# State-space setups moved within the first FFN of a hybrid decoder trunk, B and C loaded earlier, one scan split

## The chip, the cores and the metric

The kernel runs on one core of one Trainium2 chip. The metric is the device time of one execution in microseconds (us). A core has five engines that run side by side, each through its own list of instructions: TensorE (PE, matmuls; PEld is its weight load), VectorE (DVE), ScalarE (ACT), GpSimd (POOL) and SyncE (SP), which here only issues transfers. They wait for each other through semaphores, which are counters: an instruction adds to one when it is done, and another engine waits for a value.

## The reference

A trunk of two layers over 1024 tokens of width 1024, batch 1, float32. Cut to what matters:

```python
x = x + even_mixer(rms_norm(x, ...))                  # RWKV-7 and RG-LRU
x = x + conv_ffn(rms_norm(x, f_norm_g[0]), ...)       # "the first FFN"
x = x + odd_mixer(rms_norm(x, ...))                   # S5, below
x = x + conv_ffn(rms_norm(x, f_norm_g[1]), ...)
return rms_norm(x, final_norm_g)

def conv_ffn(xn, w_up, conv_w, conv_b, w_down):       # 1024 -> 2 x 2816 -> 1024
    h = causal_dwconv(xn @ w_up, conv_w, conv_b)
    gate, val = jnp.split(h, 2, axis=-1)
    return (silu(gate) * val) @ w_down

def odd_mixer(xn, w_in, A_re, A_im, log_dt, B_re, B_im, C_re, C_im, D, w_glu):
    u = xn @ w_in                                     # 64 groups of 16 channels
    a = exp((A_re + i A_im) * dt)                     # 64 complex states per group
    b_bar = (a - 1) / (A_re + i A_im) * (B_re + i B_im)
    s[t] = a * s[t - 1] + b_bar u[t]                  # over 1024 tokens
    y = gelu(Re((C_re + i C_im) s) + D * u)
    val, gate = jnp.split(y @ w_glu, 2, axis=-1)
    return val * sigmoid(gate)
```

## The kernel before, in words

Every matmul in float32 is done in three: weights and activations are each split in a high part (a ScalarE cast) and a low part (the rest, by GpSimd for weights, by VectorE for activations), and high x high, high x low and low x high are added in PSUM.

**The first FFN, up phase.** 22 pairs (i = 0 to 21), each a tile of 128 gate and 128 value columns. A pair is made by a seven-product scheme (`ORDER`, `part_pe`): 84 matmuls of 128x512. Pairs use two sets of PSUM banks in turn. The raw weights come by SP (`load_raw`, L2084), GpSimd makes sums of blocks, ScalarE the high parts (`w_hi_act`, L2107), GpSimd the low parts (`w_lo_pool`, L2111). VectorE adds the pieces and scales them (`evac_dve`, L2633), does the convolution (`conv_dve`, L2610) and the product of gate and value (`h_dve`, L2617). The finished hidden tile is stored in HBM (`hidden_sp`). Behind its own work of pair i, VectorE calls `beside_pair_dve`. Each engine works through its list in order: ScalarE's casts of the next weights stand behind its work on the evacuated banks (`begin_act`, L2375).

**The first FFN, down phase.** Hidden tiles come back from HBM (`fetch_sp`) in four groups of 7, 5, 5 and 5. In each group there are eight units (c = 0 to 7), one for each 128 output columns; a unit of group 0 is 7 x 3 x 2 = 42 matmuls of 128x512 into one of two accumulators in turn (L2257). Units 0 and 1 take their weights in two chunks (`load_chunk`, L2289), the others by `load_down` (L181), with casts (L2402, L191) and low parts (L2337, L198), all a unit ahead. After unit c VectorE adds the accumulator to the residual (L2689), splits one hidden tile for the next group (L2391), and calls `beside_dve(g, c)`.

**The state-space tables** are built beside this FFN by the class `Tables`. VectorE's steps are small, mostly on 128x32, and linked: most wait for the one before. `angles_dve(0)` copies D and an identity (20 copies, counted in `s5_clear`); `setup_dve` 0 and 1 make powers of a, 2 the factor of B, 3 `b_bar` (needs B), 4 the starts of the turning tables, 5 and 6 double those tables (`fine`, `coarse`), 7 clears two buffers and `powers_dve(0)` begins the filters. C comes by SP (`load_c_sp`), is transposed by TensorE after units 3 and 5 of group 0 (`turn_c_pe`, L2805) and copied by VectorE (`keep_c`). In groups 1 and 2 each unit carries one of 16 halves of the filters: GpSimd multiplies (`half_products_pool`, L3043, into t_mg) and sums (`half_sums_pool`, L3053, into t_gx), VectorE makes t_hx (L3099, L3109), TensorE transposes and multiplies (`half_pe`, L3121 to L3135), ScalarE keeps the result, and it goes to HBM.

**The S5 layer.** For each of eight tiles i TensorE does state matmuls (`states_pe`, L3522), filter matmuls (`filters_pe`) and output matmuls (`output_pe`, L3545), between units of the input projection. Ahead of `states_pe(i)` stand three waits: `unit_free`, `in_read` (the transfer g_in of tile i has landed, L3410) and `s5_dve` at 15 * (i - 1) + 5. VectorE's scan of a tile is 15 counted instructions: one copy, four products, an addition, a subtraction, two scans (L3751), four products, two sums. After scan 5 it also makes the low parts of four tiles of y (`g_part`, L3367).

The order of all this is written out by hand. SP's list around the change is in `load_sp`, GpSimd's in `lo_pool`.

Of the kernel before, what the change touches and what calls it, by code (L numbers as in the profile page):

```python
# [61 lines left out]
def trunk(nc, io, out):  # L62
# [1840 lines left out]
    NP = FT  # L1903
# [15 lines left out]
    class Ffn:  # L1919
# [381 lines left out]
        def load_sp(self, sp):  # L2301
            for i in range(1, NP):
                for n in ("11", "22", "12", "21"):
                    self.load_raw(sp, i, n)
                if i > 1:
                    self.hidden_sp(sp, i - 2)
            self.load_chunk(sp, 0, 0)
            for m in range(self.groups[0][1]):
                self.fetch_sp(sp, m)
            self.hidden_sp(sp, NP - 2)  # L2310
            self.load_chunk(sp, 0, 1)
            for g in range(len(self.groups)):
                fetched = list(self.next_tiles(g))
                if g:
                    self.load_chunk(sp, g, 0)
                    self.load_chunk(sp, g, 1)
                    for m in fetched[:3]:
                        self.fetch_sp(sp, m)
                    fetched = fetched[3:]
                for c in range(2, DT):  # L2320
                    self.load_down(sp, g, c)
                    if (g, c) == (0, 2):
                        self.hidden_sp(sp, NP - 1)
                        if self.tables:
                            self.tables.load_first_sp(sp, self.q_used0 + SEVEN * NP)
                    for m in fetched[:2]:
                        self.fetch_sp(sp, m)
                    fetched = fetched[2:]
                    if (g, c) == (0, 5) and self.tables:
                        self.tables.load_second_sp(sp)  # L2330
# [439 lines left out]
    class Tables:  # L2770
# [47 lines left out]
        def beside_pair_dve(self, dve, i):  # L2818
            if i == 2:
                self.angles_dve(dve, 0)  # L2820
            elif i in (4, 6):
                self.angles_dve(dve, i // 2 + 1)
            elif i in (8, 9, 10):
                self.setup_dve(dve, i - 8)
            elif i == 11:
                self.setup_dve(dve, 4)

# [4 lines left out]
        def beside_first_pool(self, pool, g, c):  # L2832
            if self.half_of(g, c) is not None:
                self.half_products_pool(pool, self.half_of(g, c))

        def beside_pool(self, pool, g, c, lo_done):
            if self.half_of(g, c) is not None:
                self.half_sums_pool(pool, self.half_of(g, c), lo_done)
            elif g > self.HALF_GROUPS[-1] and c in (2, 3):
                self.turns_pool(pool, 0, c - 2)  # L2840
# [21 lines left out]
        def beside_dve(self, dve, g, c):  # L2862
            if g == 0 and c == 1:
                self.setup_dve(dve, 5)
            elif g == 0 and c == 2:
                self.setup_dve(dve, 6)
            elif g == 0 and c == 3:
                self.setup_dve(dve, 3)
            elif g == 0 and c in (4, 6):
                self.keep_c(dve, c // 2 - 2)  # L2870
            elif g == 0 and c == 5:
                nc.vector.memset(t_gx[:, :, :, :, :], 0.0).then_inc(s5_clear, 1)
            elif g == 0 and c == 7:
                self.setup_dve(dve, 7)
# [85 lines left out]
        def double_turns(self, table, n, size):  # L2960
# [9 lines left out]
            self.square_turn()  # L2970

        def setup_dve(self, dve, c):
            run = self.link.run
# [34 lines left out]
            elif c == 4:  # L3008
# [5 lines left out]
                for _ in range(3):  # L3014
                    self.square_turn()
            elif c == 5:
                for table in (fine, coarse):
                    run(nc.vector.memset(table[:, 0, :, 0:1], 1.0))
                    run(nc.vector.memset(table[:, 1, :, 0:1], 0.0))
                for n in (1, 2, 4, 8):  # L3020
                    self.double_turns(fine, n, 16)
            elif c == 6:
                for n in (1, 2, 4):
                    self.double_turns(coarse, n, 8)
            else:
# [6 lines left out]
        def half_products_pool(self, pool, n):  # L3032
# [7 lines left out]
            if n == 0:  # L3040
                pool.wait_ge(s5_clear, 23)
            for k, (b, a) in enumerate(((0, 0), (1, 1), (1, 0), (0, 1))):
# [156 lines left out]
    with ExitStack() as sc:  # L3199
# [182 lines left out]
        with nc.Block() as block:  # L3382
# [315 lines left out]
            def _(dve):  # L3698
# [28 lines left out]

                def scan_dve(i):
                    done = 15 * i

                    def up(ins):
                        ins.then_inc(s5_dve, 1)

                    c_i, s_i = (rot[i % 2][:, :, k, :] for k in range(2))
# [10 lines left out]
                    dve.wait_ge(s5_dve, done + 4)  # L3745
                    up(nc.vector.tensor_tensor(x, x, xt, ALU.add))
                    dve.wait_ge(s5_dve, done + 5)
                    up(nc.vector.tensor_tensor(y, y, yt, ALU.subtract))
# [23 lines left out]
                for i in range(DT):  # L3772
                    scan_dve(i)
                    if i + 2 < DT:
                        scale_u(i + 2)
                    if i == DT - 3:
                        for k in range(4):
                            g_part(nc.vector, k, y_lo_dve)
# [47 lines left out]
```

## Time and profile before

| | us |
|---|---|
| median of 3 runs | 2570.85 (2568.71 to 2570.9) |
| profiled execution | 2569.76 |
| its span in the trace | 2566.3 |
| TensorE busy in it | 2461.1 (96%) |
| VectorE, ScalarE, GpSimd busy | 1463.5, 1108.4, 1307.2 |

The span is from the first to the last instruction in the trace. Times in rows are microseconds from its start. The up phase of the first FFN lies before 1204, group 0 of its down phase from there to 1289, groups 1 to 3 up to 1514, and the S5 scan ends near 1700.

### The profile page before, as it was taken

To read this page: it belongs to the slowest core of one execution; us is meant where nothing else is said; L and a number is where in the kernel's file an instruction comes from. 1 tells how busy PE (TensorE), PEld (TensorE's weight loads), DVE (VectorE), ACT (ScalarE), POOL (GpSimd) and SP (SyncE) were. 2 spreads that over 40 slices of the span, in tenths; PEclk is the share of its full clock that TensorE was granted. 3 is DMA by queue.
4 is the path that set the end of the run, shared out by engine and by line. 5 is a ranking of instruction groups with operands and counts; after the bars stand their busy time and mean duration, and the time that the engine had idled before them with its cause. 6 is when DMAs were issued, how large, how long until landed. Compare 5 with 4: busy or idle time off the path is not lost. (4 is left out here: it accounts for less than half of the span.)

```text
span 2566.3 us, 33658 instructions
## 1 busy us (share of the span) xinstructions
PE 2461.1 (96%) x12861; PEld 2049.7 (80%) x12861; DVE 1463.5 (57%) x1902; ACT 1108.4 (43%) x1782; POOL 1307.2 (51%) x1072
## 2 busy tenths in 40 slices
PE   8999899999999998999999999989999999999997
PEld 6788788888777786888778878978878888888886
DVE  6441578877556667566566546654375565562223
ACT  5442344544444543455144444433265454452222
POOL 5323445454246775875268644412367777762221
PEclk9999999999999999999999999999999999999998
DMA  3112000000111222223445424531212222243312
GB/s 107 46 39 60 21 1 2 1 1 1 42 58 58 91 74 66 83 85 126 116 167 201 139 90 144 174 106 54 61 49 88 78 82 90 75 140 107 111 50 86
DMA packets 249504, 203.46 MB, mean 79 GB/s; under 512 B 25061, under 2 KB 228359, under 8 KB 247303
## 3 DMA queue, kind: packets, MB, share of 16 engines
q1 hardware_dynamic: 235143, 179.63, 22.4%
q10 hardware_dynamic: 14208, 21.76, 2.4%
q8 instruction: 99, 1.62, 0.3%
q14 instruction: 54, 0.44, 0.1%
HBM read 148.92 MB, written 48.23 MB: 77 GB/s over the span
## 5 line engine op out<-in xcount | busy, mean ns | idle before, releaser
L198 POOL TENSOR_TENSOR dense_lo<-dense_raw,dense_hi 128x512 fp32r<-128x512 f32 (+2 forms) x142 | 175.4, 1236 | 465.9 <-ACT dense_hi L191 465.6
L191 ACT CAST dense_hi<-dense_raw 128x512 fp32r<-128x512 f32 (+2 forms) x142 | 79.3, 565 | 393.1 <-PE acc_o L1716 144.2
L2111 POOL TENSOR_TENSOR dense_lo<-w_raw_l,dense_hi 128x512 fp32r<-128x512 f32 x88 | 118.2, 1343 | 63.9 <-ACT dense_hi L2107 63.7
L2111 POOL TENSOR_TENSOR dense_lo<-w_sums_l,dense_hi 128x512 fp32r<-128x512 f32 x66 | 103.1, 1563 | 72.9 <-ACT dense_hi L2107 72.9
L2111 POOL TENSOR_TENSOR w_l<-w_raw_l,w_l 128x512 fp32r<-128x512 f32 x88 | 114.9, 1305 | 46.7 <-ACT w_l L2107 46.7
L198 POOL TENSOR_TENSOR w_lo_e<-w_raw_e,w_hi_e 128x512 fp32r<-128x512 f32 x42 | 56.4, 1345 | 158.1 <-ACT w_hi_e L191 158.1
L404 PE MATMUL main_ps<-rounded 128*128 128x256 f32 x896 | 128.1, 294 | 8.9 <-DVE rounded L299 8.9
L404 PEld LDWEIGHTS main_ps<-rounded 128*128 128x128 f32 x896 | 113.6, 190 | 27.3 <-DVE rounded L299 23.3
L2111 POOL TENSOR_TENSOR w_l<-w_sums_l,w_l 128x512 fp32r<-128x512 f32 x66 | 104.0, 1575 | 45.1 <-ACT w_l L2107 45.1
L2257 PE MATMUL bank_b<-h_hi_l,dense_hi 128*128 128x512 f32 x352 | 109.9, 394 | 6.2 <-POOL dense_lo L198 5.8
L2173 PE MATMUL acc_o<-x_early_l,dense_hi 128*128 128x512 f32 x352 | 108.7, 390 | 3.4 <-POOL dense_lo L2111 3.4
L2173 PE MATMUL bank_a<-x_early_l,w_l 128*128 128x512 f32 x396 | 104.5, 400 | 7.4 <-POOL w_l L2111 7.4
L2257 PE MATMUL bank_b<-h_lo_l,dense_hi 128*128 128x512 f32 x352 | 109.3, 392 | 0.0
L2257 PE MATMUL bank_b<-h_hi_l,dense_lo 128*128 128x512 f32 x352 | 108.8, 391 | 0.0
L2173 PE MATMUL acc_o<-x_late_l,dense_hi 128*128 128x512 f32 x352 | 108.3, 389 | 0.0
L2633 DVE TENSOR_TENSOR bank_b<-bank_b,p_kept_later_l 128x512 f32<-128x512 f32 x44 | 28.5, 695 | 139.8 <-ACT p_kept_later_l L2367 139.8
L2257 PE MATMUL bank_a<-h_hi_l,dense_hi 128*128 128x512 f32 x336 | 105.2, 394 | 2.0 <-DVE h_lo_l L2391 1.3
L2689 DVE TENSOR_TENSOR x_res<-x_res,bank_a 128x1024 f32<-128x1024 f32 x28 | 34.2, 1220 | 126.8 <-PE bank_a L2257 126.8
L2173 PE MATMUL bank_a<-x_late_l,w_l 128*128 128x512 f32 x396 | 104.0, 399 | 1.2 <-DVE x_late_l L2071 1.2
L2257 PE MATMUL bank_a<-h_lo_l,dense_hi 128*128 128x512 f32 x336 | 103.7, 390 | 0.0
L2257 PE MATMUL bank_a<-h_hi_l,dense_lo 128*128 128x512 f32 x336 | 103.5, 389 | 0.0
L2173 PE MATMUL acc_o<-x_early_l,w_l 128*128 128x512 f32 x396 | 100.9, 390 | 2.0 <-ACT p_kept_l L2367 1.9
(545 smaller groups left out, 7035.4 us busy)
## 6 DMA issues: line engine op xcount, KB each, us to landing
w_raw_l<-in_f_w_up SPq DMA_DIRECT2D x176, 256.0 KB, 3.0
hidden<-val SPq DMA_DIRECT2D x44, 512.0 KB, 2.6
h_f_l<-hidden SPq DMA_DIRECT2D x44, 512.0 KB, 4.7
w_raw_e<-in_e_w_in SPq DMA_DIRECT2D x42, 256.0 KB, 2.9
dense_raw<-in_f_w_down SPq DMA_DIRECT2D x40, 256.0 KB, 2.9
dense_raw<-in_f_w_down SPq DMA_DIRECT2D x48, 192.0 KB, 2.6
s_states<-t_hx ACTq DMA_DIRECT2D x16, 512.0 KB, 2.9
s_inputs<-t_in ACTq DMA_DIRECT2D x16, 512.0 KB, 3.0
```

The lines of the kernel that those rows point to most:

```text
L191: nc.scalar.copy(self.hi[:, par, 0:n, :], self.raw[:, par, 0:n, :]).then_inc(w_hi_done, 1)
L198: pool.tensor_tensor(self.lo[:, par, 0:n, :], self.raw[:, par, 0:n, :], self.hi[:, par, 0:n, :].bitcast(F32), op=ALU.subtract).then_inc(w_ ...
L404: return nc.tensor.matmul(bank[:, at:at + 2 * CH], lhs, rhs, skip_group_check=True, **flags)
L2111: pool.tensor_tensor(self.ring_lo[n % 4], self.source(ORDER[n % SEVEN]), self.ring_hi[n % 4].bitcast(F32), op=ALU.subtract).then_inc(q_lo, 1)
L2173: last = nc.tensor.matmul(bank, w[n % 4][:, j, :], x(j, BLOCK[k]), start=begins and j == 0 and w is self.ring_hi and x == self.x_hi, stop= ...
L2257: last = nc.tensor.matmul(self.down_acc[s][:, h * HALF:(h + 1) * HALF], place[w][:, t, :], x[here][:, h * HALF:(h + 1) * HALF], start=begi ...
L2633: nc.vector.tensor_tensor(here, here, kept, ALU.mult if kept.shape[-1] == SEQ else ALU.add).then_inc(q_evac, 1)
L2689: nc.vector.tensor_tensor(here, here, self.down_acc[c % 2][:, :], ALU.add).then_inc(unit_free, 1)
```

## The change

- SP: C (real part) and B are loaded right after unit 1's second weight chunk of group 0, and no longer after the last hidden store.
- VectorE: `angles_dve(0)` leaves pair 2, and setups 0, 1, 2 and 4 leave pairs 8, 9, 10 and 11. In group 0, unit 1 now carries setups 0 and 1, unit 2 setups 2 and 3, unit 3 the angle copies, the clearing of t_gx and setup 4, units 4 to 6 the former setups 5 and 6 in pieces beside the copies of C; unit 7 is as before.
- GpSimd: the products of the first half come after the low parts of unit 7 in group 0, and wait for 21 counts of `s5_clear` in place of 23.
- S5 scan: the scan of each tile is two functions, called one after the other; for tile 6 the low parts 2 and 3 of y come between them, and only 0 and 1 ahead.

```diff
@@ load_sp
             self.load_chunk(sp, 0, 1)
+            if self.tables:
+                self.tables.load_first_sp(sp, self.q_used0 + SEVEN * NP)
...
                     if (g, c) == (0, 2):
                         self.hidden_sp(sp, NP - 1)
-                        if self.tables:
-                            self.tables.load_first_sp(sp, self.q_used0 + SEVEN * NP)
@@ beside_pair_dve
-            if i == 2:
-                self.angles_dve(dve, 0)
-            elif i in (4, 6):
+            if i in (4, 6):
                 self.angles_dve(dve, i // 2 + 1)
-            elif i in (8, 9, 10):
-                self.setup_dve(dve, i - 8)
-            elif i == 11:
-                self.setup_dve(dve, 4)
@@ beside_first_pool, beside_pool
-            if self.half_of(g, c) is not None:
+            if self.half_of(g, c):
                 self.half_products_pool(pool, self.half_of(g, c))
...
+            elif (g, c) == (self.HALF_GROUPS[0] - 1, DT - 1):
+                self.half_products_pool(pool, 0)
@@ beside_dve
+            if g:
+                return
+            if c in (1, 2):
+                self.setup_dve(dve, 2 * c - 2)
+                self.setup_dve(dve, 2 * c - 1)
+            elif c == 3:
+                self.angles_dve(dve, 0)
                 nc.vector.memset(t_gx[:, :, :, :, :], 0.0).then_inc(s5_clear, 1)
+                self.setup_dve(dve, 4)
+            elif c == 4:
+                self.keep_c(dve, 0)
+                self.first_turns_dve()
+                for n in (1, 2, 4):
+                    self.double_turns(fine, n, 16)
+            elif c == 5:
+                self.double_turns(fine, 8, 16)
+                for n in (1, 2):
+                    self.double_turns(coarse, n, 8)
+            elif c == 6:
+                self.keep_c(dve, 1)
+                self.double_turns(coarse, 4, 8)
+            elif c == 7:
                 self.setup_dve(dve, 7)
                 self.powers_dve(dve, 0)
@@ half_products_pool
-                pool.wait_ge(s5_clear, 23)
+                pool.wait_ge(s5_clear, 21)
@@ vector list of the S5 layer
-                    scan_dve(i)
+                    scan_first_dve(i)    # copy, four products, addition
+                    if i == DT - 2:
+                        for k in range(2, 4):
+                            g_part(nc.vector, k, y_lo_dve)
+                    scan_rest_dve(i)
                     if i + 2 < DT:
                         scale_u(i + 2)
                     if i == DT - 3:
-                        for k in range(4):
+                        for k in range(2):
                             g_part(nc.vector, k, y_lo_dve)
```

`first_turns_dve` holds the four memsets that began setup 5.

## Rows read from the trace of the kernel before

**Rows 1.** The page's first part: busy time, share, instructions.
```profile
span 2566.3 us, 33658 instructions
PE 2461.1 (96%) x12861; PEld 2049.7 (80%) x12861; DVE 1463.5 (57%) x1902; ACT 1108.4 (43%) x1782; POOL 1307.2 (51%) x1072
```

**Rows 2.** Stretches of the up phase: length; busy PE, PEld, DVE, ACT, POOL; clock; DMA.
```profile
814.22:855.15 40.93, 38.66 (x170) 31.38 (x168) 27.91 (x42) 20.80 (x31) 28.01 (x23) 1.00 0.23 72
920.78:960.85 40.07, 38.67 (x170) 31.38 (x168) 26.97 (x42) 18.71 (x30) 28.30 (x23) 1.00 0.25 79
960.85:1008.49 47.64, 41.78 (x170) 33.35 (x168) 35.21 (x67) 18.52 (x29) 28.75 (x23) 0.93 0.21 67
1008.49:1051.55 43.06, 39.98 (x170) 32.59 (x168) 29.80 (x42) 19.14 (x29) 31.08 (x25) 0.96 0.23 74
1051.55:1089.63 38.08, 38.08 (x170) 31.54 (x168) 22.24 (x23) 19.11 (x28) 29.81 (x23) 1.00 0.27 84
```

**Rows 3.** Timeline behind setup 1: start, length, instruction, [idle before it and its releaser].
```profile
962.70 4.10 DVE L2895 TENSOR_TENSOR small<-power 128x32 f32<-128x32 f32 x4
...
972.59 1.20 ACT L2375 ACTIVATE gate<-acc_o,prm 128x1024 f32<-128x1024 f32 x1 [8.56 <-DVE acc_o L2633]
...
976.19 2.93 PE L2173 MATMUL bank_a<-x_early_l,w_l 128*128 128x512 f32 x6 [4.30 <-POOL w_l L2111]
```

**Rows 4.** Timelines of SP, ScalarE and TensorE in group 0.
```profile
1200.47 1.39 SPq L2289 DMA_DIRECT2D dense_raw<-in_f_w_down  x2
1212.06 4.97 SPq L181 DMA_DIRECT2D dense_raw<-in_f_w_down  x2
...
1219.30 1.51 SPq L2782 DMA_DIRECT2D c_raw<-in_o_C_re  x2
...
1224.29 3.08 SPq L2790 DMA_DIRECT2D b_raw<-in_o_B_im  x2
...
1230.61 0.98 SPq L181 DMA_DIRECT2D dense_raw<-in_f_w_down  x2
...
1219.55 0.62 ACT L191 CAST dense_hi<-dense_raw 128x512 fp32r<-128x512 f32 x1 [2.10 <-PE bank_a L2257]
...
1235.63 1.16 ACT L191 CAST dense_hi<-dense_raw 128x512 fp32r<-128x512 f32 x2 [11.49 <-DMA dense_raw<-in_f_w_down]
...
1237.73 0.78 PE L2257 MATMUL bank_b<-h_hi_l,dense_hi 128*128 128x512 f32 x2 [4.68 <-POOL dense_lo L198]
```

**Rows 5.** Timelines of GpSimd, VectorE and TensorE after group 0 ends at 1289.06.
```profile
1292.94 3.33 POOL L3043 TENSOR_TENSOR t_mg<-b_bar,power 128x256 f32<-128x256 f32 x4 [2.23 <-DVE t_fir L3029]
...
1295.82 3.49 DVE L3109 TENSOR_TENSOR t_hx<-t_mh 64x288 f32<-64x288 f32 x4
...
1299.95 1.97 PE L3121 MATMUL acc_o<-ident,t_gx 128*128 128x128 f32 x8 [2.77 <-POOL t_gx L3053]
```

**Rows 6.** Scan of tile 6: timelines; last, transfers from 1668 (count, KB, us to landing).
```profile
1670.82 0.58 SPq L3410 DMA_DIRECT2D g_in<-s_inputs  x1
...
1674.08 1.27 DVE L3744 TENSOR_TENSOR r_tmp<-bank_a,rot 128x512 f32<-128x512 f32 x2
...
1678.84 5.29 PE L3522 MATMUL bank_a<-u_now,g_in 128*128 128x128 f32 x32 [3.23 <-DVE f_hat L3751]
...
g_in<-s_inputs SPq DMA_DIRECT2D x1, 1024.0 KB, 7.9
```

**Rows 7.** Stretches behind two of the stalls, columns as in the second group.
```profile
1299.70:1303.10 3.40, 3.15 (x15) 3.16 (x16) 1.61 (x4) 1.33 (x4) 2.20 (x4) 0.51 0.48 158
1678.60:1681.90 3.30, 3.06 (x14) 3.09 (x15) 3.23 (x6) 0.00 (x0) 0.00 (x0) 0.50 0.41 101
```

**Rows 8.** Stretches of group 0 between residual additions of units 1, 3 and 7.
```profile
1223.57:1249.23 25.66, 20.98 (x87) 16.86 (x86) 18.02 (x77) 3.22 (x6) 4.54 (x4) 0.93 0.68 169
1249.23:1289.06 39.83, 39.83 (x185) 33.16 (x183) 16.98 (x20) 8.22 (x12) 8.98 (x8) 1.00 0.21 56
```

**Rows 9.** Sum over five stretches: angle copies and setups 0, 1, 2, 4.
```profile
sum 32.42, PE 32.42 PEld 26.88 DVE 30.17 ACT 6.64 POOL 17.70; mean PE 6.48 PEld 5.38 DVE 6.03 ACT 1.33 POOL 3.54
```

More of the change, by code:

```diff
@@ L2862, in beside_dve @@
         def beside_dve(self, dve, g, c):
[L2863 to L2871, printed above, removed]
-                nc.vector.memset(t_gx[:, :, :, :, :], 0.0).then_inc(s5_clear, 1)
-            elif g == 0 and c == 7:
+            if g:
[5 more added lines that the diff above has]
+                self.angles_dve(dve, 0)
+                nc.vector.memset(t_gx[:, :, :, :, :], 0.0).then_inc(s5_clear, 1)
+                self.setup_dve(dve, 4)
[12 more added lines that the diff above has]
+            elif c == 7:
                 self.setup_dve(dve, 7)
@@ L2970, in double_turns, with first_turns_dve @@
             self.square_turn()
+        def first_turns_dve(self):
+            for table in (fine, coarse):
+                self.link.run(nc.vector.memset(table[:, 0, :, 0:1], 1.0))
+                self.link.run(nc.vector.memset(table[:, 1, :, 0:1], 0.0))
         def setup_dve(self, dve, c):
@@ L3015, in setup_dve @@
                     self.square_turn()
[L3016 to L3024, printed above, removed]
             else:
@@ L3726, in scale_u, with scan_up, scan_first_dve @@
                     nc.vector.tensor_tensor(acc, acc, spread[:, :], ALU.mult).then_inc(u_scaled, 1)
[L3728 to L3732, printed above, removed]
+                def scan_up(ins):
+                    ins.then_inc(s5_dve, 1)
+                def scan_first_dve(i):
+                    done, up = 15 * i, scan_up
                     c_i, s_i = (rot[i % 2][:, :, k, :] for k in range(2))
@@ L3746, in scan_dve, with scan_rest_dve @@
                     up(nc.vector.tensor_tensor(x, x, xt, ALU.add))
+                def scan_rest_dve(i):
+                    done, up = 15 * i, scan_up
+                    c_i, s_i = (rot[i % 2][:, :, k, :] for k in range(2))
+                    x, y = f_hat[:, 0, :, :], f_hat[:, 1, :, :]
+                    xt, yt = r_tmp[:, 0, :, :], r_tmp[:, 1, :, :]
                     dve.wait_ge(s5_dve, done + 5)
```

## The prediction

> **What bounds the kernel now.** The page's first part comes first: TensorE is busy for 2461.1 of 2566.3 us [rows 1]. No other engine can be the bound as a whole, so the only time to win is the 105 us in which TensorE stands still, plus whatever its clock loses after standing. The next view is therefore TensorE's timeline with the idle time ahead of each row, and the stretches cut so that each holds equal work. The reader is to see four places.
>
> (a) Up phase. Two pairs of tiles are 168 matmuls and take 38.08 us where nothing disturbs them (170 records: the cuts take in both ends). Four other stretches with the same 170 records take 40.93, 40.07, 47.64 and 43.06 us [rows 2]. They are the pairs beside which VectorE runs the angle copies (pair 2), setup 0 (pair 8), setups 1 and 2 (pairs 9, 10) and setup 4 (pair 11). The timeline shows how: four products of setup 1 take 4.10 us, the evacuation behind them ends late, ScalarE sits 8.56 us before it may start the gate tile, its next weight cast is queued behind that, GpSimd waits for the cast, and TensorE stands 4.30 us [rows 3].
>
> (b) First down group, fourth unit. TensorE stands 4.68 us for a low part, ScalarE's cast before it 11.49 us for weights from HBM, and SP had issued these only at 1230.61, because C and B (from 1219.30) and two fetches were ahead of them [rows 4].
>
> (c) Edge of groups 0 and 1. TensorE stands 2.77 us for t_gx, whose products GpSimd began only at 1292.94, after VectorE's two memsets [rows 5].
>
> (d) Scan. TensorE stands 3.23 us before the state matmuls of tile 7 [rows 6]. The view names VectorE's scan. I read this one differently, below.
>
> Each long stall is followed by a stretch at a granted clock of 0.5, the lower of the two levels (1.2 GHz); after (c) and (d) it lasts 3.4 us [rows 7]. Such a stretch costs half its length if TensorE is busy in it.
>
> **The change, part by part.**
>
> *Setups out of the up phase.* Angle copies and setups 0, 1, 2, 4 leave pairs 2 and 8 to 11. What they cost is read from whole stretches, so that stall and low clock are both in it: 40.93 - 38.08 = 2.85; 40.07 - 38.08 = 1.99; 47.64 - 38.08 = 9.56; 43.06 - 38.08 = 4.98 [rows 2]. Sum 19.38 us, all on the path, as TensorE is followed at once by the next pair. The angle steps beside pairs 4 and 6 stay, so nothing is counted for them. I take 19.4; the bounds are 17 (a rest of short waits stays) and 19.4.
>
> *B and C ahead of the third unit's weights.* Six loads move on SP from behind the last hidden store to ahead of the weights of unit 2. Their condition (all up-phase low parts made) is met by then. In the trace the queue issues nothing there: the second weight chunk is out by 1201.9, and unit 2's first load comes at 1212.06, when GpSimd has freed its buffer [rows 4]. The six took from 1219.30 to 1227.4, 8.1 us, so they fit the 10.2 us gap. Behind them come unit 2's weights, the last hidden store and fetches of tiles 7 and 8, some 8 us earlier than now, and unit 3's weights, then released by GpSimd's low part of unit 2. So the DMA wait goes. Price of the stall with its slow clock: from the residual addition of unit 1 to that of unit 3 are 25.66 us [rows 8]. Two units of 42 matmuls at 38.08/168 = 0.2267 us are 19.04. Gain 6.6 us. What could be late instead are unit 2's weights, now behind the small packets. Unit 3's, behind the same packets and two fetches, were cast 5.0 us after their issue; at that rate unit 2's are there at 1217.1, for a cast at 1219.55 [rows 4]. Bounds of this part: 4 and 6.6.
>
> *VectorE in group 0.* This is the place where the moved work is paid. The five steps took 32.42 us in the up phase, with GpSimd busy for 17.70 us of that in 17 instructions [rows 9]. There a VectorE instruction on two operands in SBUF ends only when GpSimd's ends (four products of 32 columns in 4.10 us [rows 3]); one short instruction of 0.19 us still slips through per GpSimd instruction. Without GpSimd they are 32.42 - 17.70 + 17 x 0.19 = 17.9 us. What VectorE does now between the two ends of group 0 is 18.02 + 16.98 = 35.0 us [rows 8]. With the moved work 52.9, and some 1.5 for short gaps between linked steps: 54.4. After the gain above, the group is 65.5 - 6.6 = 58.9 us long. Spare: 4.5 us, against GpSimd's part there. GpSimd is busy 8.98 of 39.83 us there, in eight instructions of 1.1 us [rows 8]: two low parts for each unit, one in its middle, one under the residual addition, which reads PSUM and isn't held up. Six of the first kind lengthen VectorE's work by 6 x 1.1 = 6.6 at most. So VectorE ends group 0 between 4.5 early and 2 late (at the up phase's rate: 32.42 + 35.0 + 1.5 - 58.9 = 10.0 late). TensorE feels a late residual addition only a unit later, as two accumulators alternate, and the second set of C transposes, which waits for VectorE's copies of the first, comes after unit 5, when by the same durations the copies are some 3 us old. I take no stall inside the group.
>
> The Trainium skill, "SBUF — State Buffer", section "SBUF: two separate sides", says that VectorE and GpSimd share a port pair as an exclusive lock, and that the loser is blocked for the other's whole instruction. The rows on VectorE's products agree. By that rule alone the six instructions cost 6.6 us and VectorE would be 2 us late, which the next step absorbs in part.
>
> *First half of the filters.* Its products go into GpSimd's gap after the low part of unit 7 and wait for 21 counts, not for the two memsets. They took 3.33 us beside VectorE [rows 5], and GpSimd has such gaps, as just counted. Only the sums are left at the edge; they end some 5 us after it, while TensorE comes 8.1 us after it (1297.18 = 1299.95 - 2.77). Late next is VectorE's t_hx, needed 1.1 us (eight transposes) after TensorE comes, that is 9.2 after the edge. It ended 10.25 after it (1299.31), and GpSimd's products and sums ran beside it; with the 3.33 us of products gone it gains half to all of them, so it ends 6.9 to 8.6 after the edge, plus any lateness. Gain 2.77 + 3.4/2 = 4.4 [rows 5, 7], less 0.6 for lateness. Taken 3.8, bounds 0 and 4.4.
>
> *Scan of tile 6 in two parts.* The state matmuls of tile 7 wait for s5_dve at 95, which is the copy and four products of scan 6. The last of these ended at 1675.4 [rows 6], so VectorE had long released them when they began at 1678.84; the f_hat scan that ends beside them isn't awaited. They also wait for g_in of tile 7: issued at 1670.82, landed 7.9 us later, at 1678.7 [rows 6]. That is the wait. Its issue waits on the state matmuls of tile 6 and four y moves on SP, none of which is touched. The split brings the products some 2 us forward, and VectorE's total stays. So does the stall with its slow clock. Late next would be the end of scan 6, which the output matmuls need, 8.0 us after 1678.84 (5.29 of state matmuls, twelve more at 0.2267); it comes some 4 us after it, perhaps 5 after the split. Gain 0; bounds -0.5 and 4.9 (3.23 + 1.7).
>
> **Sum.** 19.4 + 6.6 + 3.8 + 0 = 29.8 us. The profiled execution took 2569.76 (span 2566.3, 3.5 around it), 1.1 below the median 2570.85. 2569.8 - 29.8 = 2540.0; on the scale of the median 2541.0.
>
> **Rivals.**
> A. The scan wait does go, as the releaser's name says: a further 3.23 + 1.7 = 4.9 us, 2536. For it, the scan's end falls within 0.03 us of TensorE's start; against it, the count awaited and the landing.
> B. VectorE's full list in group 0 makes a new stall at its edge. At the up phase's rate it is 10.0 us late: the last residual addition then holds up the second accumulator of group 1 by about 7, t_hx by 2 more, and the clock falls (1.7), 10.7 in all where 4.4 stand now: 26.0 - 6.3 = 19.7 gained, 2551. With half of that lateness, 2546.
> C. Slower: VectorE becomes the bound of group 0. If every one of some 100 moved instructions took 1.2 us there, as the four products did, they would take 120 in place of 17.9; VectorE would need 156 us for a stretch of 59, and some 97 - 30 = 67 us would be lost: 2638. It decides from (4.5 + 30)/100 = 0.35 us extra per moved instruction. It needs GpSimd busy without a gap; it is busy for 23% of the time.
> D. The up phase's stalls are not due to these steps, and stay: 10.4 gained, 2560. Against it, the undisturbed pairs differ in nothing else.
>
> **Numbers.** Forecast 0.76, A 0.09, B 0.10, C 0.02, D 0.03. The forecast's own range is 2538 to 2545. The range for 8 in 10 goes to A on one side and half of B on the other: 2536 to 2547. A measurement of this kernel tells 0.2%, 5 us. Faster by more: all but C and a rest, 0.96; same 0.02; slower 0.02.
>
> **What would show it.** TensorE's pairs 1 to 21 at 38.08 us for each two, or little more beside pair 4; no idle row from 820 to 1200. No wait at unit 3, and SP's B and C issued about 10 us before unit 2's weights. VectorE's residual additions in group 0 come behind TensorE's unit ends, by 1 to 4 us from unit 4 on; the first t_gx transposes without a wait and at full clock. The stall before the state matmuls of tile 7 still 3 us long, still ending 0.1 us after g_in lands. It is wrong if that stall is gone, or if a wait for VectorE's x_res or t_hx stands at the edge of group 1.

## The result, and the profile after

The changed kernel takes 2546.45 us (median of 5 runs, 2543.61 to 2552.49) against 2570.85 (5 runs, 2567.28 to 2574.57). The ratio is 0.9911, 95% interval 0.9897 to 0.9925: faster by 22.9 us (19.3 to 26.5), where 29.8 were forecast. Set on the median shown, the ratio gives 2548, just outside the range; the median lies inside.

The profiled execution of after took 2552.49, the longest of the five. Its first part of the page; the columns are those of [rows 1]:

```profile
span 2550.4 us, 33658 instructions
PE 2460.6 (96%) x12861; PEld 2050.4 (80%) x12861; DVE 1457.0 (57%) x1902; ACT 1109.6 (44%) x1782; POOL 1312.0 (51%) x1072
```

The spans differ by 15.9 us. TensorE runs the same 12861 matmuls in the same order in both kernels, so the start of each can be set against the start of the same one before. The difference moves by these steps:

| stretch (start times of before) | measured | forecast |
|---|---|---|
| unchanged, up to 787 | +5.0 | 0 |
| up phase, to 1050 | -19.3 | -19.4 |
| group 0, fourth unit | -6.5 | -6.6 |
| edge of groups 0 and 1, to 1304 | -0.5 | -3.8 |
| scan of tiles 6 and 7, to 1737 | +2.3 | 0 |
| unchanged, behind it | +3.2 | 0 |

The two unchanged stretches hold no edit. Most of their 8.2 us come where TensorE's clock stays low for longer behind the same waits (last section); up to 787 the other kernels of this study lie between 3.2 us earlier and 1.6 later than before. Without the two stretches the profile says -24.1, beside -22.9 from the ratio and -24.4 from the medians. So 5.7 us are missing against the forecast's stretches, 3.3 at the edge and 2.3 in the scan. The 2.3 are less firm: in four kernels whose scan has no edit the same stretch moved by +0.1 (p_setups), +0.6 (s_slots), +1.2 (p_half) and +3.6 (p_load). At the edge two kernels without an edit there, p_load and p_scan, moved by 0.2 and 0.1.

**Up phase.** Stretches of two pairs in after, first and last cut at the same matmuls as the first four of [rows 2]:

```profile
819.23:857.41 38.18, 38.18 (x171) 31.59 (x169) 22.25 (x22) 21.74 (x31) 29.84 (x23) 1.00 0.26 83
923.04:961.17 38.13, 38.13 (x170) 31.55 (x170) 23.03 (x24) 19.33 (x30) 31.04 (x25) 1.00 0.27 83
961.17:999.25 38.08, 38.08 (x170) 31.54 (x169) 22.25 (x23) 19.10 (x28) 29.83 (x23) 1.00 0.27 84
999.25:1037.33 38.08, 38.08 (x170) 31.54 (x169) 22.25 (x23) 19.10 (x28) 29.84 (x23) 1.00 0.26 83
```

40.93, 40.07, 47.64 and 43.06 have become 38.18, 38.13, 38.08 and 38.08. TensorE is busy for the whole of each, at full clock.

**Unit 3.** SP's timeline in after, which answers to [rows 4]:

```profile
1187.58 1.58 SPq L2782 DMA_DIRECT2D c_raw<-in_o_C_re  x2
...
1193.30 3.06 SPq L2790 DMA_DIRECT2D b_raw<-in_o_B_im  x2
...
1197.84 4.97 SPq L181 DMA_DIRECT2D dense_raw<-in_f_w_down  x2
...
1207.35 4.07 SPq L181 DMA_DIRECT2D dense_raw<-in_f_w_down  x2
```

B and C are out by 1196.4, before unit 2's weights (1197.84); unit 3's follow at 1207.35, where before has them at 1230.61: 23.3 us earlier, of which 14.2 are the kernel's lead by then. From there to 1272 TensorE has no idle row.

**VectorE in group 0.** Stretches between its residual additions of units 1 to 7 in after, columns as in [rows 8]:

```profile
1209.36:1219.31 9.95, 9.95 (x45) 8.25 (x44) 9.15 (x51) 1.51 (x3) 2.33 (x2) 1.00 0.64 213
1219.31:1229.62 10.31, 10.31 (x51) 8.61 (x51) 9.80 (x21) 2.88 (x5) 3.04 (x3) 1.00 0.28 96
1229.62:1242.34 12.72, 12.72 (x58) 10.53 (x57) 11.38 (x40) 2.39 (x4) 3.16 (x3) 1.00 0.38 91
1242.34:1253.31 10.97, 10.97 (x54) 9.17 (x53) 10.00 (x38) 2.09 (x3) 2.34 (x2) 1.00 0.16 46
1253.31:1266.55 13.24, 13.24 (x60) 10.96 (x59) 12.73 (x32) 2.60 (x4) 5.88 (x7) 1.00 0.10 30
1266.55:1274.20 7.65, 5.75 (x26) 4.43 (x24) 7.41 (x14) 1.56 (x5) 4.34 (x5) 1.00 0.39 114
sum 64.84, PE 62.94 PEld 51.96 DVE 60.47 ACT 13.03 POOL 21.09; mean PE 10.49 PEld 8.66 DVE 10.08 ACT 2.17 POOL 3.52
```

An addition that isn't late starts 0.20 us after the first matmul of the next unit (unit 1: 1209.16 and 1209.36). By that mark TensorE ends units 1 and 7 at 1209.36 and 1268.26, 58.9 us apart, as forecast. VectorE needs 64.8 for its list and never waits for TensorE in it. Its additions of units 2 to 7 stand 0.4, 1.2, 3.5, 5.0, 7.8 and 5.9 us behind the ends of their units (the expectations below put the last at 5.5). The fifth stretch is the worst; there the new products of the first half of the filters run. GpSimd's timeline in after, then VectorE's:

```profile
1259.39 1.02 POOL L198 TENSOR_TENSOR dense_lo<-dense_raw,dense_hi 128x384 fp32r<-128x384 f32 x1 [2.57 <-ACT dense_hi L191]
1260.36 2.41 POOL L3046 TENSOR_TENSOR t_mg<-b_bar,power 128x256 f32<-128x256 f32 x4
...
1270.00 3.56 POOL L3056 TENSOR_TENSOR t_gx<-t_mg 64x256 f32<-64x256 f32 x4
```
```profile
1259.49 0.97 DVE L2897 TENSOR_TENSOR small<-small 128x32 f32<-128x32 f32 x1
1260.49 1.17 DVE L2902 TENSOR_TENSOR coarse<-coarse,small 128x32 f32<-128x32 f32 x2
1261.56 1.26 DVE L2902 TENSOR_TENSOR s_tmp<-coarse,small 128x32 f32<-128x32 f32 x2
1262.85 0.34 DVE L2902 TENSOR_TENSOR coarse<-coarse,s_tmp 128x32 f32<-128x32 f32 x2
```

The same pair of 32 columns takes 0.34 us when GpSimd is still, and 1.17 and 1.26 beside its products. The sums of the first half (1270.00) run beside VectorE's list too, since VectorE is still at it when group 0 ends on TensorE. Setting each step against the shortest of its line and shape in this trace gives an estimate of the hold-ups up to the addition of unit 7: 7.9 us beside low parts, 1.9 beside the products and 1.8 beside the sums, 11.6 in all. What this costs TensorE, from its timeline in after:

```profile
1275.47 0.74 PE L2257 MATMUL bank_b<-h_hi_l,dense_hi 128*128 128x512 f32 x2 [3.17 <-DVE x_res L2689]
...
1279.73 1.03 PE L3124 MATMUL acc_o<-ident,t_gx 128*128 128x128 f32 x8
...
1280.99 0.43 PE L3130 MATMUL acc_o<-d_diag,ident 128*128 128x64 f32 x2 [0.22 <-DVE t_hx L3112]
```

The transposes of t_gx, which waited 2.77 us [rows 5], start at once. In place of that wait the second accumulator of group 1 waits 3.17 us for VectorE's addition of unit 7.

**Scan.** SP, VectorE, TensorE in after, and the transfer issued at 1649.74 (last column: us from issue to landing); they answer to [rows 6]:

```profile
1649.74 0.58 SPq L3413 DMA_DIRECT2D g_in<-s_inputs  x1
...
1650.30 1.28 DVE L3746 TENSOR_TENSOR r_tmp<-bank_a,rot 128x512 f32<-128x512 f32 x2
...
1659.24 5.74 PE L3525 MATMUL bank_a<-u_now,g_in 128*128 128x128 f32 x32 [4.76 <-issue]
...
g_in<-s_inputs SPq DMA_DIRECT2D x1, 1024.0 KB, 9.4
```

VectorE's products are done at 1651.6, TensorE stands until 1659.24, and g_in lands at 1659.15. The wait has not gone; it has grown from 3.23 to 4.76, with a landing time that has grown from 7.9 to 9.4.

### The profile page after: what moved, and what is told of

Same layout as the page of the kernel before. It is cut to its first block and busy times, and to the rows that moved or that the text cites. A ratio compares the mean times of both kernels' runs of the same rounds, so it can differ in the third digit from the quotient of the medians.

```text
span 2550.4 us, 33658 instructions
## 1 busy us (share of the span) xinstructions
PE 2460.6 (96%) x12861; PEld 2050.4 (80%) x12861; DVE 1457.0 (57%) x1902; ACT 1109.6 (44%) x1782; POOL 1312.0 (51%) x1072
## 5 line engine op out<-in xcount | busy, mean ns | idle before, releaser
L404 PEld LDWEIGHTS main_ps<-rounded 128*128 128x128 f32 x896 | 114.1, 191 | 28.0 <-DVE rounded L299 23.3
L2633 DVE TENSOR_TENSOR acc_o<-acc_o,p_kept_later_l 128x512 f32<-128x512 f32 x44 | 28.6, 695 | 133.6 <-ACT p_kept_later_l L2367 133.5
L220 PE MATMUL acc_e<-xn_hi_e,w_hi_e 128*128 128x512 f32 x320 | 101.0, 397 | 1.2 <-POOL w_lo_e L198 1.2
```

What stands on the lines that cost most here:

```text
L220: last = nc.tensor.matmul(acc[:, h * HALF:(h + 1) * HALF], w[:, par, j, :], x[:, k + j, h * HALF:(h + 1) * HALF], start=first, stop=final)
L404: return nc.tensor.matmul(bank[:, at:at + 2 * CH], lhs, rhs, skip_group_check=True, **flags)
L2633: nc.vector.tensor_tensor(here, here, kept, ALU.mult if kept.shape[-1] == SEQ else ALU.add).then_inc(q_evac, 1)
```

## Experiments

Two theories. By the first, the gains lie where the forecast put them, and the missing part is VectorE's lateness in group 0, from steps that take longer there than the ledger said; the scan's wait is for g_in. By the second, the parts disturb each other elsewhere (the transfers moved, the clock), or the scan's wait is VectorE's, as its name in the profile said. All ratios are against the kernel before on the same chip.

**The four parts alone.** `p_setups` has only the new places of VectorE's steps, `p_load` only the early B and C, `p_half` only the early products of the first half, `p_scan` only the split.

```diff
p_setups: beside_pair_dve, beside_dve, setup_dve, first_turns_dve as after
p_load:   load_sp as after
p_half:   half_products_pool(pool, 0) behind the low parts of unit 7; wait_ge(s5_clear, 21)
p_scan:   scan_first_dve, low parts 2 and 3, scan_rest_dve as after
```

> Only the setups move (VectorE's lists of the change; B and C, the first products and the scan as before). Theory (VectorE's list is the wait in the up phase, and group 0 still holds 6.6 us of DMA wait in which VectorE can catch up): the up phase is 19.4 us shorter, the stall at unit 3 stays near 4.7 us, the edge of groups 0 and 1 stalls for 2.8 to 5 us as GpSimd's products come late as before: in all 17 to 19.4 us faster, 0.9925 to 0.9935. Rival (the up phase's stalls have another cause): under 5 us faster.

> Only B and C are loaded early. Theory: the wait for unit 3's weights goes with its slow clock, 6.6 us faster (0.9974), nothing new elsewhere. Rival (unit 2's weights become late): a wait of 1 to 3 us before unit 2, 4 to 5 us faster.

> Only the first half's products go ahead of the edge. Theory (in the kernel before, VectorE has idle time in units 6 and 7, so GpSimd's four products cost it nothing that matters): the 2.77 us wait and the slow clock behind it go, 3.5 to 4.4 us faster (0.9984). Rival (the products hold up VectorE whatever its load): a wait for x_res or t_hx at the edge, 0 to 2 us faster.

> Only the scan of tile 6 is split. Theory (TensorE waits for g_in of tile 7 to land): the stall before the state matmuls of tile 7 stays between 3 and 5 us and ends 0.1 us after the landing; time unchanged within 1.5 us. Rival (TensorE waits for VectorE's scan, as the releaser's name says): the stall goes, 4.9 us faster (0.9981).

| | median (runs) | ratio, interval | us of 2570.85 |
|---|---|---|---|
| p_setups | 2552.85 | 0.9931, 0.9915 to 0.9948 | -17.7 |
| p_load | 2565.20 | 0.9972, 0.9961 to 0.9983 | -7.2 |
| p_half | 2566.17 | 0.9981, 0.9972 to 0.9990 | -4.9 |
| p_scan | 2571.42 | 1.0002, 0.9992 to 1.0012 | +0.5 |

They add up to -29.3 us, nearly the forecast's -29.8. Together they bring 22.9. The intervals of the four, taken together, leave some 6 us of doubt in that sum (an estimate), so whole times alone don't show that something is lost between the parts; the start times do, at the edge. There p_setups loses 2.2 us, p_half gains 4.5, p_load and p_scan stay within 0.2. The sum would be a gain of 2.3, and after gains 0.5. So of the 3.3 us missing there, about half comes with the setups alone and about half from setups and products together. TensorE's idle rows of p_setups, of p_half and of p_scan:

```profile
1216.87 1.14 PE L2257 MATMUL bank_b<-h_hi_l,dense_hi 128*128 128x512 f32 x2 [5.19 <-POOL dense_lo L198]
1280.65 1.97 PE L3122 MATMUL acc_o<-ident,t_gx 128*128 128x128 f32 x8 [4.34 <-POOL t_gx L3054]
...
1660.10 5.44 PE L3523 MATMUL bank_a<-u_now,g_in 128*128 128x128 f32 x32 [3.56 <-DMA g_in<-s_inputs]
```
```profile
1235.39 1.19 PE L2257 MATMUL bank_b<-h_hi_l,dense_hi 128*128 128x512 f32 x2 [4.85 <-POOL dense_lo L198]
...
1674.17 5.44 PE L3524 MATMUL bank_a<-u_now,g_in 128*128 128x128 f32 x32 [4.11 <-DMA g_in<-s_inputs]
```
```profile
1678.49 1.83 PE L3522 MATMUL bank_a<-u_now,g_in 128*128 128x128 f32 x7 [3.68 <-issue]
```

With the setups alone the wait for t_gx grows from 2.77 to 4.34: VectorE, although it had unit 3's stall to catch up in, is still 2.0 us late at the addition of unit 7 and clears its buffers later, and the products wait for that. With the early products alone the edge is 4.5 better, as forecast (4.4), for VectorE isn't late. In p_load the fourth unit gives -6.5, and the wait for t_gx stays at 2.76. Both p_setups and p_half leave VectorE's scan as it was, and the profile now names g_in, where it named f_hat before: the name changes from kernel to kernel, the wait doesn't. In all 13 kernels that have this transfer the state matmuls of tile 7 start 0.1 us after it lands.

**VectorE's lateness.** `a_half_back` is after with the first half's products where before had them (21 counts kept). `a_unit0` is after with setup 0 beside unit 0.

```diff
a_half_back, beside_first_pool and beside_pool:
-            if self.half_of(g, c):
+            if self.half_of(g, c) is not None:
-            elif (g, c) == (self.HALF_GROUPS[0] - 1, DT - 1):
-                self.half_products_pool(pool, 0)
a_unit0, beside_dve:
-            if c in (1, 2):
-                self.setup_dve(dve, 2 * c - 2)
-                self.setup_dve(dve, 2 * c - 1)
+            if c == 0:
+                self.setup_dve(dve, 0)
+            elif c in (1, 2):
+                if c == 2:
+                    self.setup_dve(dve, 2)
+                self.setup_dve(dve, 2 * c - 1)
```

> The changed kernel with one part undone: the first half's products again at the edge of groups 0 and 1 (still waiting for 21 counts). Theory (GpSimd's four products beside units 6 and 7 hold up VectorE's small steps): VectorE's residual addition of unit 7, 5.5 us late in the changed kernel, comes 2.5 to 4 us earlier, TensorE's 3.17 us wait for x_res goes, and at most 1 us for t_gx comes: 1 to 3 us faster than the changed kernel, 0.9893 to 0.990 of the kernel before. Rival (the list of moved steps alone is too long): the wait for x_res stays near 3 us, and a wait for t_gx comes on top, 0 to 3 us slower than the changed kernel.

> The changed kernel with setup 0 beside unit 0, where VectorE is idle for 2.86 us, and no longer beside unit 1. Theory (VectorE is the wait at the edge, and every us taken off its list counts): the addition of unit 7 comes 2.9 us earlier, inside the 4.1 us that TensorE allows; the x_res wait falls from 3.17 to under 0.5 us: about 3 us faster than the changed kernel, 0.989 of the kernel before. Rival (a steady limit, as contention grows to fill it): unchanged.

a_half_back: 2542.85 (2540.71 to 2545.29), ratio 0.9902 (0.9887 to 0.9917). a_unit0: 2545.38 (2544.44 to 2547.37), ratio 0.9909 (0.9894 to 0.9925). TensorE's idle rows at the edge, of a_half_back; then VectorE's addition of unit 2 and TensorE's wait in a_unit0:

```profile
1265.81 0.73 PE L2257 MATMUL bank_b<-h_hi_l,dense_hi 128*128 128x512 f32 x2 [1.79 <-DVE x_res L2689]
...
1279.98 1.09 PE L3122 MATMUL acc_o<-ident,t_gx 128*128 128x128 f32 x8 [0.83 <-POOL t_gx L3054]
```
```profile
1215.44 1.22 DVE L2689 TENSOR_TENSOR x_res<-x_res,bank_a 128x1024 f32<-128x1024 f32 x1 [1.37 <-PE bank_a L2257]
...
1272.00 0.73 PE L2257 MATMUL bank_b<-h_hi_l,dense_hi 128*128 128x512 f32 x2 [3.17 <-DVE x_res L2689]
```

VectorE is 1.4 us less late (3.17 falls to 1.79), less than the 2.5 to 4 us expected, and the result lies between theory and rival. GpSimd's timeline in a_half_back says why, with VectorE's addition of unit 7 below it:

```profile
1261.73 2.50 POOL L3044 TENSOR_TENSOR t_mg<-b_bar,power 128x256 f32<-128x256 f32 x4
1264.37 3.21 POOL L3054 TENSOR_TENSOR t_gx<-t_mg 64x256 f32<-64x256 f32 x4
```
```profile
1264.53 1.22 DVE L2689 TENSOR_TENSOR x_res<-x_res,bank_b 128x1024 f32<-128x1024 f32 x1
```

The products come one low part later and still run beside VectorE's list, all four of them. What has left the list is the sums, which start when it ends. By the same estimate as above the hold-ups beside the sums fall from 1.8 us to none, and those beside the products from 1.9 only to 1.6. The edit doesn't take the products away from VectorE, as it was meant to, and what they cost in that place was not measured by a run. The first transposes of t_gx don't wait here either, for TensorE is already late by x_res. The 0.83 us at 1279.98 are of the second half, for which after waits 0.85 at its place. The edge is 1.3 us better than in after by start times. The medians of after and a_half_back can't be told apart by the intervals; the rows can.

a_unit0 was a miss. Time freed ahead of unit 2's end isn't kept: VectorE arrives early at the addition of unit 2, stands 1.37 us for TensorE, and everything behind is as in after, to the same 3.17. Lateness builds up from the third unit on; work must go from there to a place with idle time.

**The list moved up.** `a_shift` is after with each unit of group 0 carrying what the rows of after show room for.

```diff
a_shift, beside_dve (group 0; unit: after -> a_shift)
-  0: -          1: setups 0, 1    2: setups 2, 3   3: copies, t_gx, setup 4
+  0: setup 0    1: setups 1, 2    2: setup 3, copies   3: t_gx, setup 4, first turns, fine 1
-  4: keep_c 0, first turns, fine 1, 2, 4   5: fine 8, coarse 1, 2   6: keep_c 1, coarse 4
+  4: keep_c 0, fine 2, 4          5: fine 8, coarse 1      6: keep_c 1, coarse 2, 4
```

> The changed kernel with VectorE's list in group 0 moved up as a whole: setup 0 beside unit 0, 1 and 2 beside unit 1, 3 and the copies beside unit 2, and so on; the same instructions in all. Theory (VectorE has 59 us in group 0 after unit 1, needs 65, and the 2.86 us of idle time beside unit 0 count only if everything behind it moves up too): the addition of unit 7 comes 2.5 to 3 us earlier than 5.5 late, the x_res wait of 3.17 us falls below 0.7, 2.5 to 3 us faster than the changed kernel, 0.990 of the kernel before. Rival (the wait follows GpSimd's products beside unit 7 and nothing before them): unchanged.

Measured: 2541.22 (2540.50 to 2542.49), ratio 0.9874 (0.9857 to 0.9890). VectorE from the addition of unit 1 to that of unit 7, and TensorE at the edge and in the scan:

```profile
1205.20:1265.66 60.46, 60.46 (x276) 50.26 (x275) 56.65 (x177) 11.90 (x19) 18.05 (x19) 1.00 0.28 81
```
```profile
1266.93 0.72 PE L2257 MATMUL bank_b<-h_hi_l,dense_hi 128*128 128x512 f32 x2 [0.60 <-DVE x_res L2689]
...
1281.28 1.09 PE L3129 MATMUL acc_o<-ident,t_gx 128*128 128x128 f32 x8 [0.85 <-POOL t_gx L3061]
...
1650.80 6.27 PE L3530 MATMUL bank_a<-u_now,g_in 128*128 128x128 f32 x32 [4.69 <-issue]
```

The wait for x_res is 0.60, as expected: the addition of unit 7 is 3.4 us late in place of 5.9, and TensorE can bear 2.8. The edge is 2.3 us better than in after by start times. The first theory's cause at the edge is shown: the same work, begun earlier so that VectorE is less late, gives most of that wait back. The whole time fell by more, 5.2 us between the medians; the ratio is below the 0.990 expected, and these rows don't say where the rest comes from.

**The scan's wait.** `b_no_gin7` is before without the transfer of tile 7's inputs g_in; the state matmuls of tile 7 use tile 6's. `b_cover` is before with twelve matmuls of the GLU ahead of the state matmuls of tile 7.

```diff
b_no_gin7, the issue of g_in and its wait:
+                    if i == DT - 1:
+                        return
-                pe.wait_ge(in_read, 16 * (i + 1))
+                pe.wait_ge(in_read, 16 * min(i + 1, DT - 1))
b_cover:
-                states_pe(DT - 1)
                 place_products(pe, 0, 2, 4, g_ready).then_inc(w_used, 1)
+                states_pe(DT - 1)
```

> The kernel before, and the transfer g_in of tile 7 left out (tile 7 is computed with tile 6's inputs). Theory (TensorE waits for that landing): the stall before the state matmuls of tile 7 falls from 3.2 to under 0.3 us, 4 to 5 us faster (0.9982). Rival (it waits for the scan on VectorE): the stall stays at 3.2 us but for what lighter traffic gives, unchanged.

> The kernel before, with twelve matmuls of the first gate unit (2.7 us) ahead of the state matmuls of tile 7 and no longer behind them. Theory (a landing at a fixed time): 2.7 of the 3.2 to 3.7 us are covered and the clock doesn't fall, 2.7 to 4.4 us faster (0.9986). Rival (scan on VectorE ends the wait, at the same moment): the same; what tells them apart is the other kernel of this call, this one is to show that the stall can be had back by order alone.

b_no_gin7: 2566.30, ratio 0.9985 (0.9973 to 0.9998). b_cover: 2568.26, ratio 0.9990 (0.9980 to 1.0000). The state matmuls of tile 7 in b_no_gin7, which have no idle time before them, with the next wait; and those of b_cover:

```profile
1677.59 3.81 PE L3524 MATMUL bank_a<-u_now,g_in 128*128 128x128 f32 x32
...
1684.87 3.81 PE L3547 MATMUL bank_b<-s_prev,hx 128*128 128x128 f32 x32 [0.72 <-DVE s_prev L3766]
```
```profile
1681.79 3.81 PE L3522 MATMUL bank_a<-u_now,g_in 128*128 128x128 f32 x32 [1.29 <-issue]
```

Without the transfer the wait is gone with VectorE untouched, and the 32 matmuls take 3.81 us in place of 5.29 [rows 6], 5.74 in after and 6.27 in a_shift, which all stand behind an idle stretch: the clock [rows 7]. The second theory's reading of the scan falls. By start times b_cover is 3.2 us better from 1304 to 1737.

**Other places for the setups.** `s_slots` is before with early B and C and the moved setups in pieces within pairs 9 to 19, ahead of the second evacuation; `s_all` adds the early products and the cover.

```diff
s_slots, in VectorE's list of a pair, behind h_dve(i - 1):
+            self.tables.slot_pair_dve(dve, i)
   # pairs 9 to 12 copies, 13 setup 0, 14 and 15 powers, 16 and 17 factor, 18 starts, 19 turns
s_all: s_slots + the early products (as p_half) + the cover (as b_cover)
```

> The kernel before with B and C early, and the angle copies and setups 0, 1, 2 and 4 in pieces beside pairs 9 to 19 of the up phase, but ahead of the evacuation for which VectorE waits 4.8 us and more, and no longer behind it. Theory (the setups cost in the up phase because of their place in VectorE's list, not because of their length): no stall in the up phase (19.4) and none at unit 3 (6.6), the edge stalls for 2.8 us as before: 26 us faster, 0.990. Rival (any such work in the up phase holds up a weight cast): stalls of about 1 us beside each of the eleven pairs, 10 to 16 us faster, 0.995.

> The kernel of s_slots with the first half's products ahead of the edge and twelve matmuls ahead of the state matmuls of tile 7 as well. Theory: the parts add up, as VectorE isn't full in group 0: 26 + 4.4 + 3 = 33 to 34 us faster, 0.987, with no wait at the edge. Rival (parts compete as in the changed kernel): 26 to 28 us, 0.990.

s_slots: 2556.61 (2554.64 to 2558.65), ratio 0.9936 (0.9921 to 0.9951). s_all: 2551.03 (2545.68 to 2552.83), ratio 0.9913 (0.9898 to 0.9928). Both miss their expectations. VectorE, ScalarE and TensorE around the powers of pair 15 in s_slots:

```profile
1075.39 4.96 DVE L2906 TENSOR_TENSOR small<-power 128x32 f32<-128x32 f32 x4
...
1085.20 1.21 ACT L2375 ACTIVATE val<-acc_o,prm 128x1024 f32<-128x1024 f32 x1 [7.97 <-DVE acc_o L2633]
...
1090.66 2.93 PE L2173 MATMUL bank_a<-x_early_l,w_l 128*128 128x512 f32 x6 [3.26 <-POOL w_l L2111]
```

It is the stall of [rows 3] again, four products of 4.96 us included. The copies (pairs 9 to 12) and setup 0 (pair 13) pass without a wait; the powers (pairs 14 and 15) and the factor (16 and 17) bring waits of 2.98, 3.26, 1.43 and 0.57 us, and 12.5 us by start times. In the up phase GpSimd works for 28 to 31 us of each two pairs [rows 2], and four linked steps take 4.96 us where they take 0.50 beside a still GpSimd. In s_all, where group 0 doesn't hold the moved setups, the early products bring 4.5 us at the edge, as in p_half: this supports that in after it is VectorE's full list that takes the gain.

**The best of both.** `best` is a_shift with the cover, and with the scan in one piece again.

> The kernel with VectorE's list of group 0 moved up (0.9874 of before), with two edits more: 12 matmuls of the GLU (place_products(0, 2, 4)) ahead of the state matmuls of tile 7, and the scan of tile 6 in one piece again, since those matmuls need the low parts 2 and 3 of y, which the split puts behind the four products. If the wait before the state matmuls of tile 7 is for the transfer g_in, the twelve matmuls (3 us at full clock) fill it: the 4.7 us wait falls to 1 to 2, the clock behind it stays up for longer, and the time falls by 2.6 to 4.5: ratio 0.986 (0.9855 to 0.9865), some 2538. Rival: the scan in one piece brings its end, which the output matmuls need, late enough to give the gain back: 0.9874, the same as without the two edits. Should the twelve matmuls wait for low parts, a wait for a_lo stands ahead of them and the ratio is above 0.988.

Measured: 2539.89 (2538.07 to 2546.11), ratio 0.9889 (0.9873 to 0.9906). TensorE's state matmuls of tile 7 and the output matmuls behind them:

```profile
1648.70 3.81 PE L3530 MATMUL bank_a<-u_now,g_in 128*128 128x128 f32 x32 [0.28 <-issue]
...
1652.88 3.81 PE L3553 MATMUL bank_b<-s_prev,hx 128*128 128x128 f32 x32 [0.36 <-DVE s_prev L3772]
```

The wait is 0.28 us, the clock stays up (3.81), the twelve matmuls wait for no low part, and by start times the stretch from 1514 to 1737 is 5.8 us shorter than in a_shift. The wait did better than expected and the ratio missed: 0.9855 to 0.9865 was expected. The median is 1.3 below a_shift's and the ratio 0.0015 above it, on another chip: whole times don't tell the two apart, and that the 5.8 us reach the end is not shown. Both beat the kernel before and have lower medians than after.

## Why the prediction was wrong, by its steps

*Setups out of the up phase: right.* 19.4 forecast, 19.3 measured, and the four stretches are at 38.08 to 38.18. Rival D is out.

*B and C early: right.* 6.6 forecast, 6.5 measured in after, and the same in p_load. That it fits to 0.1 is in part luck: three kernels that keep this stall (p_half, p_scan, b_cover) took 1.4 to 1.8 us longer over it than the profile of before, from which the 6.6 was read.

*VectorE in group 0: this step failed.* The text had VectorE "between 4.5 early and 2 late" and took 0.6 us for its lateness. It was 5.9 late. By terms: the list was put at 17.9 + 35.0 = 52.9 us of work, and 60.5 were busy, 7.6 more, where the hold-ups by GpSimd were set at 6.6 at most. By the estimate above the hold-ups were 11.6, and the list without them some 49: the work was put 4 us too long, which hid part of the miss. Three things were left out of the count of hold-ups. One low part per unit was taken to fall under the residual addition, which reads PSUM; this holds only for a VectorE that is on time (in after the addition of unit 6 starts at 1266.55, long after the low part at 1259.39, and a linked step took that hold-up, 0.97 us). The first half's products are four more instructions of GpSimd, put in the same stretch by the same change; the prediction spoke of GpSimd's gap for them and not of VectorE, which took 1.17 and 1.26 us for two pairs of steps beside them. And the sums were "left at the edge", which a late VectorE hasn't reached when they run. The gaps between steps were 64.84 - 60.47 = 4.4 us, where 1.5 had been allowed: there are 114 of them, nearly all of 0.03 to 0.04 us. 7.6 + 4.4 - 1.5 = 10.5 above the forecast's 54.4.

The "No stall inside the group" held, by two accumulators, and the forecast said where a wait would show if it was wrong: x_res at the edge of group 1. It stood there with 3.17 us. That is rival B at about half its lateness (5.9 of 10.0 us), to which the text gave its share of 0.10. That its 2546 and the 2546.45 measured agree so well is luck: this rival has 5 us lost, all of them at the edge, and the rows have 3.3 there and 2.3 in the scan. The interval from 4.5 early to 10.0 late was at hand; the value was taken from its early half, while the rate of the up phase, though from a busier place, was the only row in which these very steps had been timed.

*First half of the filters: right alone, lost together.* p_half gives 4.5 at the edge; after gives 0.5. The products do come early, t_gx is on time, and VectorE takes its place as the late one: a_shift, with VectorE less late, and s_all, with the setups elsewhere, have the gain back in part and in full.

*Scan: the reason right, the size not quite.* The wait is g_in's, as b_no_gin7 shows; p_scan is level (1.0002). In after the wait is 1.5 us longer, since g_in took 9.4 us to land and not 7.9, and the stretch lost 2.3 us where the lower bound was 0.5 lost. The five kernels with the split had landings of 8.2 to 9.7 us (p_scan 8.4), the eight without it 7.7 to 9.0. p_load has no split and lost 3.6 us in this stretch, more than after. So the split isn't needed for such a loss; what sets the landing time stays open.

## What to carry to other kernels

When linked small steps move beside another engine's work, add up that engine's whole time in the new stretch, also what the same change puts there and what slides in if the list runs late, and a gap per step; then hold the sum against the stretch as it will be after the stall in it has gone. Slack is worth having only behind the last point at which the moved engine waits for someone: time freed earlier turns into idle time. A wait with several conditions goes to the one whose landing fits its end, whatever name the profile gives it; follow each condition to its row.

## What the runs showed of the hardware

VectorE's steps with both operands in SBUF end together with GpSimd's instruction beside them: in after a step started at 1259.49 ends at 1260.46, GpSimd's low part at 1260.41; one started at 1239.46 took 1.06 us and not 0.19. The residual additions, which read one operand from PSUM, aren't held up: those at 1219.31 and 1229.62 in after have a low part beside them and take 1.22 us, as without one. The Trainium skill, "SBUF — State Buffer", section "SBUF: two separate sides", states an exclusive lock, and lets VectorE take it with instructions in a two-port mode or with two inputs in SBUF; the rows agree, for the steps named and for the additions.

The 1024 KB of g_in for tile 7 took 7.9 us to land in before and between 7.7 and 9.7 in the other kernels, while small moves of y share the queue in the same microseconds.

A wait of one length doesn't always bring the clock down. In a stretch that no edit touches, TensorE waits 2.57 us in before and in after; the first row is before's, the second after's:

```profile
304.03 1.22 PE L404 MATMUL main_ps<-rounded,a_zb 128*128 128x256 f32 x8 [2.57 <-ACT rounded L596]
```
```profile
305.43 2.08 PE L404 MATMUL main_ps<-rounded,a_zb 128*128 128x256 f32 x8 [2.57 <-ACT rounded L596]
```

The same eight matmuls take 1.22 us there and 2.08 here. The mean granted clock is 1.00 from 303.5 to 306 in before and 0.50 from 305 to 308 in after. Such places move the start times of unchanged work by 1 to 3 us each, so a gain of that size is read from the rows of its own place and not from the span.
